# Border to the convolution: weight sums of the second pair, the last tile's norm, and the order of pair loads and stores of sums on SyncE's queue

## The reference

```python
h = layer_norm(DN_ALPHA * h + out, ln_g[0], ln_b[0])        # end of layer 0: "residual" and "norm"
b_gate, c_gate, u, z = jnp.split(h @ w_in, 4, axis=-1)      # 1024 -> 4096
cu = jnp.pad(c_gate * u, ((0, 0), (CONV_K - 1, 0), (0, 0)))
conv = cu[:, 0:L] * conv_w[0] + cu[:, 1:1 + L] * conv_w[1] + cu[:, 2:2 + L] * conv_w[2]
out = (b_gate * conv * jax.nn.silu(z)) @ w_out
```

## Time and profile before

| what | us |
|---|---|
| median of three executions | 2605.08 |
| the profiled execution's own time | 2612.59 |
| its span from the first to the last instruction | 2610.8 |
| parts P and B, and part C | up to 1768.2 |
| part D, products of the 48 pairs | 1768.2 to 2427 |
| part E | 2427 to 2610.8 |
| 336 products of 1.90 us in part D | 638 |

### The profile page before, as it was taken

How to read it: one execution, slowest core, us unless ns; L and a number is a source line. 1 busy time by engine, 2 the same in 40 slices (tenths; PEclk the granted TensorE clock), 3 DMA queues, 4 the chain that set the end, 5 groups by cost and what they waited for, 6 DMA issues and landing times. The chain is left out here.

```text
span 2610.8 us, 48054 instructions
## 1 busy us (share of the span) xinstructions
PE 2554.8 (98%) x17333; PEld 2403.7 (92%) x17333; DVE 1887.8 (72%) x3886; ACT 1442.5 (55%) x3529; POOL 429.4 (16%) x203
## 2 busy tenths in 40 slices
PE   8999999999999999999999999998999999999998
PEld 7999999989999999999999987888999999999787
DVE  6546651149898889898889986688877666666766
ACT  4434332248888888888888871125445445444210
POOL 0000000013344545444444400000000000000000
PEclk9999999999999999999999999999999999999999
DMA  6555454312243343333333316755544543553443
GB/s 207 188 170 183 145 157 128 94 52 45 52 100 82 83 83 83 88 82 75 87 75 82 75 44 199 225 171 195 202 178 156 201 152 130 185 188 135 143 145 112
DMA packets 245937, 337.85 MB, mean 129 GB/s; under 512 B 86338, under 2 KB 182482, under 8 KB 233234
## 3 DMA queue, kind: packets, MB, share of 16 engines
q1 hardware_dynamic: 227874, 326.40, 42.3%
q10 hardware_dynamic: 17840, 8.52, 1.1%
HBM read 225.34 MB, written 109.51 MB: 128 GB/s over the span
## 5 line engine op out<-in xcount | busy, mean ns | idle before, releaser
L1282 DVE TENSOR_TENSOR b_pt_lo<-b_transposed,b_pt_hi 128x384 fp32r<-128x384 f32 (+4 forms) x784 | 428.9, 564 | 50.8 <-ACT b_pt_hi L1172 47.4
L1267 DVE TENSOR_REDUCE ground<-b_ring 128x1 f32<-128x384 f32 (+7 forms) x784 | 409.0, 527 | 61.2 <-PE b_ring L45 47.8
L1172 ACT ACTIVATE b_pt_hi<-b_transposed 128x384 fp32r<-128x384 f32 (+4 forms) x784 | 382.2, 501 | 121.4 <-PE b_transposed L1207 110.1
L1159 ACT ACTIVATE ground<-b_ring,ground 128x384 f32<-128x384 f32 (+7 forms) x784 | 435.7, 560 | 19.4 <-DVE ground L1272 11.5
L1207 PE MATMUL b_transposed<-identity,ground 128*128 128x128 f32 (+2 forms) x2448 | 380.4, 272 | 10.2 <-DVE b_pt_lo L1282 6.4
L1207 PEld LDWEIGHTS b_transposed<-identity,ground 128*128 128x128 f32 (+2 forms) x2448 | 280.1, 134 | 58.4 <-issue 28.4
L43 PE MATMUL b_ring<-region 128*128 128x384 f32 (+7 forms) x784 | 300.5, 383 | 4.5 <-ACT ground L1159 3.2
L43 PE MATMUL p_banks<-p_x_hi,big 128*128 128x258 f32 x896 | 254.9, 285 | 11.2 <-DVE big L591 8.4
L45 PE MATMUL b_ring<-region 128*128 128x384 f32 (+7 forms) x784 | 257.9, 329 | 0.0
L44 PE MATMUL b_ring<-region 128*128 128x384 f32 (+7 forms) x784 | 257.6, 329 | 0.0
L45 PE MATMUL p_banks<-p_x_hi,big 128*128 128x258 f32 x896 | 254.9, 285 | 0.0
(11 more groups left out here) (215 smaller groups left out, 6382.8 us busy)
## 6 DMA issues: line engine op xcount, KB each, us to landing
ground<-x_a SPq DMA_DIRECT2D x23, 1032.0 KB, 6.0
ground<-w_conv SPq DMA_DIRECT2D x32, 512.0 KB, 3.8
c_tiles<-w_conv SPq DMA_DIRECT2D x32, 512.0 KB, 3.8
c_ln<-weight_sums SPq DMA_DIRECT2D x16, 1024.0 KB, 7.4
c_tiles<-weight_sums SPq DMA_DIRECT2D x16, 1024.0 KB, 7.1
weight_sums<-c_tiles SPq DMA_DIRECT2D x9, 1024.0 KB, 3.9
keys<-ground SPq DMA_DIRECT2D x64, 129.0 KB, 5.7
queries<-ground SPq DMA_DIRECT2D x64, 129.0 KB, 2.9
```

The source lines that it names most:

```text
L1159: nc.scalar.activation(p[0:rows, n % PSLOTS, 0:w], banks[0:rows, n % RING, 0:w], ACT.Exp, bias=nmax[0:rows, tile % 8:tile % 8 + 1], accum_ ...
L1172: nc.scalar.activation(turned(pt_hi, g, u, nb)[:, :, tile_columns(u, j)], tb[:, n % 2, 0:nb, 0:rows], ACT.Copy).then_inc(pt_hi_done, 1)
L1267: ins = nc.vector.tensor_reduce(top, bank[0:rows, 0:w], AX, ALU.max, negate=(chunks == 1))
L1282: nc.vector.tensor_tensor(lo, tb[:, n % 2, 0:nb, 0:rows], hi.bitcast(F32), ALU.subtract).then_inc(pt_split, 1)
```

## The change

In pass 0 on VectorE the sums of pair 1 are no longer made where SECOND_AT says, but by a table: the sum for weight 5 at step 2 ahead of the residual of the last tile, weight 6 at step 3, weights 7 and 3 at step 5. The root of the last tile goes to step 6 on ScalarE, the norm to step 7 on VectorE, with the first sum of pair 2 directly behind it; the transposes go behind product (1, 2), step 10. On SyncE's queue the sums of pair n are stored in iteration n, behind the load of pair n + 2, and the last tile's rows in iteration 1. For n = 14 and 15 the store goes ahead of the wait for its own landing and of the load.

```diff
-TURN_16 = (1, 6)
-
-SUM_16, ROOT_16, NORM_16 = 2, 3, 5
+TURN_16 = (1, 2)
+
+SUM_16, ROOT_16, NORM_16 = 2, 6, 7
+SUMS_1_AT = {2: (5,), 3: (6,), 5: (7, 3)}
@@ SyncE, loop over n
                 if n + 2 >= PER_PASS:
                     sp.wait_ge(w_split, max(W_AT[n, m] for m in W_SUM))
-                if PER_PASS <= n + 2 < PER_PASS + 2:
+                if PER_PASS - 2 <= n < PER_PASS:
+                    keep_sums(n)
                     sp.wait_ge(sums_out[sum_buffer(n)], sums_stored(n))
                 load_pair(n + 2)
                 if n < 0:
                     keep_sums(0)
                     continue
-                if n == 0:
+                if 0 < n < PER_PASS - 2:
+                    keep_sums(n)
+                if n == 1:
                     store(LAST_C)
-                if n + 1 < PER_PASS:
-                    keep_sums(n + 1)
@@ VectorE, loop over the steps
                 if i in SECOND_AT:
                     weights_lo(1, SECOND_AT[i])
+                if i == NORM_16:
+                    norm(LAST_C)
+                    sum_weights(2, SUM_PART_AT[1])
+                if next_of(n) is not None:
+                    weights_lo(next_of(n), m)
+                for part_1 in SUMS_1_AT.get(i, ()):
+                    sum_weights(1, part_1)
                 if i == SUM_16:
                     residual(LAST_C)
-                if i == NORM_16:
-                    norm(LAST_C)
-                if next_of(n) is not None:
-                    weights_lo(next_of(n), m)
-                if SECOND_AT.get(i + 1) in W_SUM:
-                    sum_weights(1, SECOND_AT[i + 1])
-                if n and n + 1 < PER_PASS and m in SUM_PART_AT:
+                if n and n + 1 < PER_PASS and m in SUM_PART_AT and (n, m) != (1, 1):
                     sum_weights(n + 1, SUM_PART_AT[m])
```

## The result

The change makes the kernel slower: median 2614.53 us of 8 executions against 2605.39 of 8 of the kernel before, ratio 1.0044 with a 95% interval of 1.0034 to 1.0054, so +8.9 to +14 us; the two medians differ by 9.1 us. I had forecast +7.2 us, with 0.53 of the chance inside 0.3% (7.8 us) and 0.42 on slower. The median lies in my range, but the price was put too low: the term for the pass border, 7.5 us, measured 8.6, and the clock and what lies behind the border, which I had put at 0, came on top.

What follows compares the result with a forecast made beforehand. TensorE, busy 98% of the span, was taken as the bound, so time changes only where it idles, at two borders. First border -0.3 plus pass border +7.5 gave +7.2 us, a median of 2612.3 us, range 2607 to 2616.

Steps and rivals of the forecast that it cites:

- the pass border: From pass 0 to pass 1: late stores of sums delay the loads of pairs 16 and 17, +7.5 us (6.8 to 8.6).
- the clock: TensorE's clock halving after idle, behind (1,7) or (16,7): counted as 0, with +1.5 us kept as the other end.
- (a): First border, VectorE: the sum for (1,5), moved ahead of the residual, waits 1.7 us for the store of sums 0.
- (b): First border, VectorE: norm moved from step 5 to 7; c12 of pair 0 at 1796.2, product (1,7) 1.9 us later.
- (d): First border, step 18: product (2,7) starts 0.3 us earlier, bounds 1.4 us gained to 1.8 us lost.
- SyncE's queue in pass 0: Loads ahead of stores of sums in pass 0: shorter loads nobody waits for, later stores covered, 0 us.
- Behind the pass border: Pairs after 17: no stores of sums there, so they just move along, 0 us.
- (1): Rival: slower, +8.7 to +9.3 us, by the pass border plus a second clock fall or late transposed rows; chance 0.22.
- late landing of the transposed rows: First border: ScalarE's first tap waits for a 7.1 us landing instead of 3.7; 2.1 us more.
- (2): Rival: the sum of (1,5) doesn't wait, first border gains 1.4 us, the whole +6 us, 2611; chance 0.13.
- (3): Rival: faster, four idle stretches of 7.9 us vanish and the pass border is free, 2597 us; chance 0.05.
- (4): Rival: nothing moves as both delays hide, 2605 us; chance 0.03.

Runs made afterwards that it cites:

- e4: Changed kernel plus 24 throwaway matmuls on TensorE around the transposes, ahead of product (1,7): stage 666.9 us, ratio 1.0016 to 1.0035 to the kernel before.
- e13: Kernel before, unchanged, profiled a third time: convolution stage 657.5 us; no timed ratio.
- e12: Kernel before, unchanged, profiled a second time: convolution stage 656.3 us; no timed ratio.
- e8: Kernel before with raw weight blocks loaded early from pair 16 on, only the sums' load waiting for their splits: stage 653.9 us, ratio 0.9983.
- e3: Changed kernel with the stores of sums 14 and 15 back in the iteration before: stage 660.3 us, ratio 1.0000 to the kernel before.
- e2: Kernel before with only SyncE's changed queue, engine lists as before: stage 668.9 us, ratio 1.0042.
- e5: Changed kernel plus 24 throwaway matmuls on TensorE right ahead of product (16,2): stage 669.5 us, ratio 1.0033 to 1.0065 to the kernel before.
- e1: Changed lists of VectorE, ScalarE and TensorE with SyncE's queue as before the change: stage 657.3 us, ratio 0.9999 to the kernel before.
- e9: Kernel before with raw blocks loaded early and the changed engine lists, stores as in the old queue: stage 655.6 us, ratio 0.9982.
- e10: Changed kernel with the last tile's residual ahead of the sum for (1,5) again: stage 666.6 us, ratio 1.0023 to 1.0054 to the kernel before.
- e11: Kernel before with raw blocks loaded early and two VectorE moves (convolution of pair 0, sum for (2,6)) later: stage 650.7 us, ratio 0.9973.
- e14: Changed kernel, unchanged, profiled a second time: convolution stage 667.8 us; no timed ratio.
- e7: Changed kernel with only the store of sums 15 late, that of 14 back an iteration: stage 667.3 us, ratio 1.0012 to 1.0033 to the kernel before.

## Why the prediction was wrong in size, point by point

- **(a) The sum of (1,5) waits for the store of sums 0**: right. 1.25 us of idle, 1.7 forecast; the 1.01 us at step 6 went, the 0.48 us at step 8 became 1.67 (1.4 forecast).
- **(b) c12 and (1,7) later**: right. c12 at 27.7 us from the stage's start, 28.0 forecast; (1,7) at 28.9, 1.6 us later than before, 1.9 forecast.
- **(d) (2,7) 0.3 us earlier**: at full speed it is, in e4, by 0.4 us. In three profiles of the changed kernel it came 0.8 to 1.0 us later, because the clock fell around (1,7), which I had counted as 0 and kept as the other end: this is a step that failed. The mean time from the stage's start to (15,1) hides it, 206.5 us in the three profiles of the kernel before and 206.6 in the three of the changed one, since a fall came at (2,7) in one of the three of before (e13, 208.2 us). With the other traces that have the same lists and no wait for the last rows, it is 205.6 or 205.7 us in three of the four with the old lists (before, e12 and e8, not e13) and 206.4 to 207.3 in all nine with the changed lists; the means differ by 0.6 us. That the sum of the term came near -0.3 is luck in part.
- **SyncE's queue in pass 0, 0 us**: right with the changed lists, within 0.1% (e3). With the old ones the late store of the last rows costs 1.9 us at (2,7) (e2), a wait that I had not looked at.
- **The pass border, 7.5 us**: the mechanism was right and the size too small. This is the main step that failed. From (15,1) to (17,1) the means are 28.5 us before and 37.2 changed, +8.6, and ScalarE's start on pair 17, counted from (15,1), moved by 8.6 us too. Two numbers of the sum were wrong. The load of pair 16 was credited with 0.7 us (9.05 to 8.35) for the lack of the store of sums 15 beside it; but 9.05 was the slowest of the three of before (9.05, 8.15, 7.68, mean 8.3), and the changed kernel's took 8.0, 9.1 and 8.1, mean 8.4. There was nothing to credit. I had also overlooked that another store moves to this place: with no store of sums 15 in between, the gates of finished outputs (L1564, 338 KB) are issued 0.5 us behind the load, where before it was 6.1 us.

```profile
1969.69 0.43 SPq L1553 DMA_DIRECT2D c_ln<-weight_sums  x1
1970.16 0.43 SPq L1564 DMA_DIRECT2D g_t<-c_ht  x1
```

In the eight traces with this store 0.5 to 0.7 us behind the load of the sums the load took 7.8 to 9.0 us from its first issue to its landing, mean 8.5; in the five with the old order 7.6 to 9.0, mean 8.0. No run tested it alone. And the store of sums 15 was taken at 4.1 us, from two that took 3.9 and 4.3; at this place it took 5.2, 3.8 and 5.2, mean 4.7. With the measured means the sum is 4.2 + 0.1 + 4.7 = 9.0 us, near the 8.6 found. The signs hold too: TensorE idle 2.35 us before (15,7) (2.8 forecast) and 5.16 before (16,2) (5). Before (16,7) it idled 0.24 us and not 2, as (16,2) ran at half speed; at full speed, in e5, it is 1.91.
- **Behind the pass border, 0 us**: the means differ by 0.8 us (422.6 and 423.4). Half speed at the last products, around 2425, is in one profile of three of before and in all of the changed kernel. But it is also in those of e1, e3, e8 and e9, in which sums 14 and 15 are not stored late, so the late stores are not needed for it. Why it comes in some executions and not in others is open.

Together: forecast -0.3 + 7.5 + 0 = 7.2; found about 0.1 + 8.6 + 0.8 = 9.5. With a bound at 7.8 us this decides between "slower" and "within 0.3%", and the medians of the timed runs, +9.1 us, agree. The ratio's middle, +11.5 us, is more than the profiles explain; its lower end is not.

Of the rivals, (1) is nearest: slower than forecast, with the clock at half speed around (1,7). But its pass border of 7.5 us was too small as well, and its late landing of the transposed rows didn't happen (2.9 us). (2) was tried by e10, and without the wait (1,7) gains 0.5 us only. (3) and (4) fall with ScalarE's 5.61 and 8.32 us.

## What to carry to other kernels

A wait that costs nothing in a trace can be free only because its DMA was issued long before; moving the issue next to the wait puts the whole landing, here 3.8 to 5.5 us each time, on the path. Where loads feed an engine that idles for them, first ask which part of the load has to wait for the trigger: splitting off the 0.75 MB that needn't brought more here (ratio 0.9983) than the reordering of engine lists, in e1 (0.9999) or on top of it in e11 (0.9973). And take a duration that carries the forecast from several executions or several like rows: the one at hand may be the slow one.

## What the runs showed that I had not expected

- 24 needless matmuls on TensorE made (2,7) come 1.4 us earlier, as the clock stayed up around (1,7); the ratio is 1.0025 (1.0016 to 1.0035) against the change's 1.0044 (1.0034 to 1.0054).
- A store of 1 MB with no load issued beside it takes 3.8 us in some executions and 5.2 to 5.5 in others at the same place: sums 15 took 3.8 in e4, e5 and e14, and 5.2 to 5.5 in the first and third profile of the changed kernel, e2, e7 and e10. That of sums 14 took 4.2 us in the changed kernel each time. The cause is open.
- Each fall of the clock lasted 3.4 or 6.8 us, and the same idle stretch does not bring one each time: around the 3.31 us before (1,7) of the kernel before it fell in e12 and not in the other two profiles. With the changed lists it fell there in all nine traces.
